# 640 unused bytes ahead of `x_piece`, so that all split operands begin 128 bytes past a multiple of 2048

## What is computed

```python
x = layer_norm(alpha * x + concat([gla(x), short_conv(x), cross_attn(x, mem)]) @ w_out, ln1_g, ln1_b)
x = layer_norm(alpha * x + square(relu(x @ w_ff1)) @ w_ff2, ln2_g, ln2_b)
```

## Time and profile before

| | |
|---|---|
| median of 3 runs | 2223.73 us (2220.53 to 2224.12) |
| the profiled execution | 2220.34 us, its span 2218.6 us |
| PE busy | 2146.5 us, 97% of the span |
| weight loads (PEld) | 1725.5 us, 78% |
| VectorE busy | 1382.3 us, 62% |
| ScalarE busy | 1011.8 us, 46% |
| GpSimd busy | 523.6 us, 24% |
| mean granted clock of TensorE | 0.991 |

### The profile page before, as it was taken

One profiled execution on the slowest core, in us unless ns is written; L12 is line 12 of the kernel. 1 busy time (PEld: TensorE's weight loads), 2 busy tenths in 40 slices (PEclk: granted clock), 3 DMA queues, 4 the chain that ended last, 5 costly groups with the idle time before them and its releaser, 6 DMA issues.

```text
span 2218.6 us, 26638 instructions
## 1 busy us (share of the span) xinstructions
PE 2146.5 (97%) x10240; PEld 1725.5 (78%) x10240; DVE 1382.3 (62%) x1902; ACT 1011.8 (46%) x1360; POOL 523.6 (24%) x483
## 2 busy tenths in 40 slices
PE   7999999999999999889999999999999999999996
PEld 5787787778877877678888788888788888778884
DVE  4667566756675666845645766666475644864458
ACT  4535344445444444454545655444443333633334
POOL 3002000200110113120100244444494900620004
PEclk9999999999999999999999999999999999999998
DMA  6122324323332332264554776867968666665563
GB/s 192 58 57 77 114 68 133 93 89 95 115 99 82 109 120 95 67 216 163 192 192 157 264 285 247 283 229 274 333 218 285 197 195 194 212 228 196 191 195 137
DMA packets 241054, 374.12 MB, mean 169 GB/s; under 512 B 16368, under 2 KB 117776, under 8 KB 240928
## 3 DMA queue, kind: packets, MB, share of 16 engines
q1 hardware_dynamic: 212096, 272.68, 37.5%
q0 software_dynamic: 28832, 99.74, 12.7%
HBM read 272.74 MB, written 99.61 MB: 168 GB/s over the span
## 4 chain that ended last, share of the span: by engine, by line
PE 78%; DVE 10%; ACT 4%; issue 4%; DMA 4%; POOL 0%; DVEq 0%; SPq 0%; ACTq 0%; POOLq 0%
PE main L68 15%; PE main L70 15%; PE main L69 15%; PE sc L68 6%; PE sc L69 6%; PE sc L70 6%; DVE w_lo L1564 3%; PE sc L542 2%; DMA raw<-in_w_in_dram 1%; PE ob L599 1%; PE aux L68 1%; PE ob L68 1%; PE aux L69 1%; PE ob L69 1%; PE aux L70 1%
## 5 line engine op out<-in xcount | busy, mean ns | idle before, releaser
L1564 DVE TENSOR_TENSOR w_lo<-w_b,w_hi 128x1024 fp32r<-128x1024 f32 x144 | 216.5, 1506 | 251.2 <-ACT w_hi L1534 251.1
L1564 DVE TENSOR_TENSOR w_lo<-raw,w_hi 128x1024 fp32r<-128x1024 f32 x144 | 207.6, 1446 | 124.0 <-ACT w_hi L1534 124.0
L1534 ACT ACTIVATE w_hi<-raw 128x1024 fp32r<-128x1024 f32 x144 | 152.4, 1059 | 248.0 <-PE main L70 112.5
L1534 ACT ACTIVATE w_hi<-w_b 128x1024 fp32r<-128x1024 f32 x144 | 152.3, 1058 | 176.9 <-PE aux L70 78.5
L1050 DVE TENSOR_TENSOR w_lo<-raw,w_hi 128x1024 fp32r<-128x1024 f32 x116 | 141.5, 1227 | 141.4 <-ACT w_hi L753 140.0
L68 PE MATMUL main<-xT_lo,w_hi 128*128 128x512 f32 (+1 forms) x528 | 219.3, 415 | 1.5 <-DVE xT_lo L1062 1.5
L70 PE MATMUL main<-xT_hi,w_hi 128*128 128x512 f32 (+1 forms) x528 | 207.7, 393 | 0.0
L69 PE MATMUL main<-xT_hi,w_lo 128*128 128x512 f32 (+1 forms) x528 | 207.3, 393 | 0.0
L68 PE MATMUL sc<-x_lo,w_hi 128*128 128x512 f32 x448 | 178.6, 399 | 8.2 <-DVE x_lo L1507 5.7
L68 PE MATMUL main<-x_lo,w_hi 128*128 128x512 f32 x448 | 178.9, 399 | 7.7 <-ACT z L1885 5.7
L68 PE MATMUL main<-w_lo,w_hi 128*128 128x512 f32 x448 | 175.3, 391 | 6.0 <-DVE w_lo L1564 5.9
(11 more groups left out here) (255 smaller groups left out, 4745.6 us busy)
## 6 DMA issues: line engine op xcount, KB each, us to landing
raw<-in_w_in_dram SPq DMA_DIRECT2D x80, 512.0 KB, 3.7
h_dram<-z SPq DMA_DIRECT2D x64, 512.0 KB, 3.7
raw<-h_dram SPq DMA_DIRECT2D x112, 256.0 KB, 2.7
w_b<-h_dram SPq DMA_DIRECT2D x112, 256.0 KB, 2.6
h_dram<-h_s SPq DMA_DIRECT2D x48, 512.0 KB, 4.8
rows<-in_x_dram POOLq DMA_DIRECT2D x32, 512.0 KB, 4.8
raw<-in_w_out_dram SPq DMA_DIRECT2D x32, 512.0 KB, 3.7
raw<-in_w_ff_dram SPq DMA_DIRECT2D x32, 512.0 KB, 6.8
```

The costliest lines, as they stand in the source:

```text
L1534: act.activation(ff.w_hi[:, n % RING, :], slot_tile(ff, m), ACT.Copy).then_inc(ff.hi_done, 1)
L1564: dve.tensor_tensor(ff.w_lo[:, n % RING, :], slot_tile(ff, m), ff.w_hi[:, n % RING, :].bitcast(F32), ALU.subtract).then_inc(ff.lo_done, 1)
```

## The change

One tile of 160 float32 values a partition is allocated ahead of `x_piece` and never used.

```diff
         ff.rstd = sb("f_rstd", [P, NT])
         ff.nmean = sb("f_nmean", [P, NT])
+        sb("to_2048", [P, 160])
         x_piece = sb("x_piece", [P, 1024])
```

## The result

The changed kernel takes 2208.14 us (median of 4 runs, 2205.84 to 2211.22) against 2223.33 us before (4 runs, 2220.53 to 2224.12) on the same chip: ratio 0.9935, 95% interval 0.9918 to 0.9952, so 15.2 us less. Measured once more for comparison with the experiments it was 0.9943 (0.9928 to 0.9959). The forecast was 2198 in a range of 2190 to 2226: the direction holds, the products do settle on the shorter step, and the gain is two thirds of the forecast's 23.7 us.

The account below looks back on a forecast made before the run. The prediction took the kernel to be bound by how fast TensorE issues 512-column products. Savings of 12.5 us (expansion) and 11.2 us (mixer) summed to 23.7 us, giving 2198 us after allowing for run spread, range 2190 to 2226.

Parts of the forecast that it names:

- Rival (a): All stages: placement is not what separates them, so no change, 2221 to 2224 us; chance 0.21 together with rival (d).
- Rival (b): Expansion: only part of the products settle; if half change, 12 us less, 2211 us; chance 0.08.
- Rival (c): Expansion and mixer: products settle on a slower step, +5 us (2229) up to +33 us (2257); chance 0.13.
- Term 1: Expansion: 5.7 ns saved on each of 2190 chain products, 12.5 us; 15.3 if all 2688 count.
- Term 2: Mixer: 5.7 ns saved on each of some 1960 chain products, 11.2 us; between 0 and 15.3.
- Term 3: Contraction: both operands stay in `w_hi`/`w_lo`, nothing moves, 0; its waits for `w_lo` stay.
- Term 4: ScalarE and VectorE copies and transfers with moved tiles: 0 for VectorE, transfers under 1 us in all.
- rival (d): Transfers of moved tiles get slower, 0.5 to 1 us, no change by itself; chance 0.21 together with rival (a).

Follow-up runs that it names:

- e1: The kernel before with 128 unused bytes ahead of `x_piece` in place of the change's 640: 2211.1 us, with the kernel before at 2228.1.
- e2: The kernel before with 384 unused bytes ahead of `x_piece` in place of the change's 640: 2210.1 us, with the kernel before at 2228.1.
- e5: The change plus 1408 unused bytes ahead of `raw`, moving `w_hi`/`w_lo` and everything behind together: 2205.3 us beside 2220.6 before.
- e6: The change plus 64 unused bytes ahead of `raw`, moving `w_hi`/`w_lo` and everything behind together: 2209.7 us beside 2220.6 before.
- e7: The kernel before with 672 unused bytes ahead of `x_piece` in place of the change's 640: 2226.0 us where the kernel before took 2220.6.
- e10: The change itself, measured again against the kernel before on the same chip: 2208.05 us, ratio 0.9943.
- e8: The kernel before with 640 unused bytes ahead of `x_hi` alone, moving only the expansion's tiles: 2208.97 us, ratio 0.9941.
- e9: The change with 384 more unused bytes ahead of `x_hi`, putting `x_hi` and `x_lo` 128 off again: 2222.77 us, ratio 1.0005.

## Why the prediction came out as it did

**The mechanism** was right, and was read from rows of before: a stage whose two operands have the ring's residues runs at 226.7 ns, the others at 232.3. After the change the expansion does too, and the mixer's products come down to 227.4 to 228.5. Rival (a) (placement does not matter) fell with the change itself and with e1, e2, e5 and e6. Rival (b) (a half settles) fell with 1149 of 1149 matmuls in the window. Rival (c) (a slower step) did not come true at 640 bytes, but exists: with 672 bytes the products are slower than with none, 233.3 ns. The reasoning "only the rest by 512 can be at work" was too narrow, 256 is enough; it did not touch the sum. The Trainium skill's account that speaks against the change, two independent read ports of a TensorE that never waits, "SBUF — State Buffer", section "Who interferes with whom", does not hold here: the same matmuls follow each other at 226.8 or 233.3 ns (e1 and e7) by nothing but the distance of their operands, and the measurement decides. The 215.8 ns of the prediction stand in the Trainium skill, "TensorE: Matmul & The Clock Gate", section "Back-to-back issue gap", for a single isolated matmul; the shortest step of any stage here is 226.8 ns.

**Term 1**, the expansion: 12.5 us forecast (up to 15.3), 11.0 measured (650.6 to 639.6), 10.3 in e10, 11.4 in e8. The saving per product was right, 5.6 ns (232.4 to 226.8). All the stage's products got shorter, 2688 x 5.6 = 15 us, and PE's idle time in the stage grew by 3.8 us, at the wait for x above all. So the chain's count of 2190 products came near, in the place of a price for that wait.

**Term 2**, the mixer: this is the step that failed. 11.2 us were forecast on the path. PE's products did get shorter in total, by 11.3 us over 2433 intervals (565.8 to 554.5 us), but the mixer ended 3.6 us earlier, and nothing that can be measured is left at the end (e9: 1.0005, 0.9994 to 1.0015). Four things were left out. A saving of 5.7 ns was taken for all products, but after each interruption, of which the mixer is full, PE needs up to ten products to settle: the mixer's steps are 227.7 (xT moving), 227.4 (xT as weights) and 228.5 ns (y), 4 to 5.4 ns less than before. The chain of waits shows what was late last, not by how much: where PE is ahead by a microsecond VectorE, ScalarE or a load of `raw` is late next; the products' share of the chain fell from 47.7 to 38.9%, and PE's idle time in the mixer rose from 28.8 to 34.0 us. Behind the stage stand two more waits that take back part of any lead, 1.7 to 3.7 us at the wait for x. And the sum has no term for the clock: in the change it fell to half for 3.4 us in the mixer where it had not, and in e9 for 10.2 us at the three places together. How much of the mixer's gain each of the four took is not told apart run by run. The prediction named the sign of this ("if the products go to 389 and the mixer does not get shorter, term 2 is wrong") and gave it no price but the lower bound of the forecast's own range, 0 for the mixer. That the total still fell well inside the range is owed to its width.

**Term 3**, the contraction: forecast 0. Its products are unchanged, but in the profile after its first waits grew from 1.6 to 4.0 us, PE was at half clock for 6.8 us behind them (up to 3.4 us of loss, none before), and the stage grew by 5.5 us; in e10, with waits of 1.8 us and no half clock there, by 0.8. By the prediction's own sign a changed contraction would have spoken against its reason; its step of 226.9 ns says that the reason is another, in the transfers and the clock. So the sum of the profiles is 3.6 + 11.0 - 5.5 = 9.1 us, and 13.1 in e10 (3.6 + 10.3 - 0.8), against 15.2 and 14.5 by the medians.

**Term 4**, other engines: 0 as forecast. VectorE was busy 1383.5 us after and 1382.3 before, ScalarE 1012.6 and 1011.8. The 0.1 us between `raw` and `w_b` in rival (d) is no price of unaligned transfers: in e5 both tiles begin at a multiple of 256, and both loads land in 2.7 us (median), as after the change, where neither does. No run shows such a price.

## What to carry to other kernels

When one kind of matmul runs at two speeds in two stages of a kernel, compare where its operands lie before anything else, and keep the distance of moving operand and weights at a multiple of 256 bytes; it cost one unused tile and gave 0.65%. Price a saving on the busiest engine by the stage: count it on the chain, then look behind the stage for the next point whose time is set by transfers, because there it is given back. A longer wait can also bring half a clock behind it, so look at the granted clock there. Those points are then the next thing to mend; here that took some 5 us more off, though not clear of noise by much.

## What was not expected of the hardware

- The step of an fp32r product of 128 x 128 weights and 512 columns by the distance of its two operands, rest by 256: 0: 226.8 ns; 32: 233.3; 64: 229.0 (ring as weights, moving operand 64 past) or 233 (ring moving, 64 short); 128: 232.4. All at the granted clock 1.00 of 2.4 GHz, in the expansion, and the 233 in the mixer. At half clock no difference is seen: 427 ns from start to start in the first products of the expansion before (928 us) and after (924 us).
- It is not a fixed surcharge for each product but a pattern: at 128 the distances of starts repeat as 228, 230, 233, 241, 232, 231, 232 ns over seven products (1400 us in the trace of before), at 0 they are 226 or 227 throughout, and after a wait they take up to ten products to get there.
- With 256 moving columns (the products of mem from 20 to 28 us) the kernel before shows a beat of five, 115, 118, 122, 120, 119 ns, with a mean of 119; after the change every distance is 120 ns. So there the multiple of 256 gives an even step, but not a faster one. There are 96 such products, of no weight in the sum.
- With the change the clock falls to half in more places than before: 56 us of the span instead of 44, at places where PE waits longer than it did (3.5 us instead of 2.1 at 784 us). A gain in products ahead of such a wait can so cost time behind it.
